# The first two mixers of a transformer stack: score and value products of two heads at once in halves of the matmul array

## The reference

```
p   = softmax(q k^T * scale, causal)              per head
o_a = g0 * p_cmp v_cmp + g1 * p_slc v_slc + g2 * p_win v_win
y_a = heads of o_a side by side;  y_b = heads of p_moba v_moba
merged = gate_a * (y_a @ w_up_nsa) + gate_b * (y_b @ w_up_moba)
x = x + g_m * (merged @ w_out)
```

## Time and profile before

| | |
|---|---|
| median of 3 runs | 2048.45 us (2046.79 to 2048.81) |
| profiled execution, its own time | 2048.88 us |
| its span in the profile | 2047.0 us |
| granted clock of TensorE, mean | 0.998 |
| loop of the first mixer, first score to the last transposes of y | 88.38 to 234.01 us |
| loop of the second mixer | from 531.41 us |

### The profile page before, as it was taken

How to read it: one execution, slowest core, us unless ns; L and a number is a source line. 1 busy time by engine, 2 the same in 40 slices (tenths; PEclk the granted TensorE clock), 3 DMA queues, 4 the chain that set the end, 5 groups by cost and what they waited for, 6 DMA issues and landing times. The chain is left out here.

```text
span 2047.0 us, 32169 instructions
## 1 busy us (share of the span) xinstructions
PE 1998.6 (98%) x12934; PEld 1775.0 (87%) x12934; DVE 1465.8 (72%) x2326; ACT 1093.2 (53%) x1732; POOL 23.6 (1%) x46
## 2 busy tenths in 40 slices
PE   7999999999999999999999999999999999999999
PEld 4889898898788988898888779888898899899888
DVE  7887778867786686567766676677667757767774
ACT  3555545535656455545545656655455536855552
POOL 1001000000010000000000000000000000000000
PEclk9999999999999999999999999999999999999999
DMA  9455458856455466555556324355555554235554
GB/s 353 157 205 196 167 181 275 273 207 187 145 201 211 147 224 206 185 186 185 186 190 201 125 102 144 130 187 187 186 177 187 186 181 137 93 124 163 187 175 134
DMA packets 266212, 372.23 MB, mean 182 GB/s; under 512 B 8400, under 2 KB 160336, under 8 KB 266064
## 3 DMA queue, kind: packets, MB, share of 16 engines
q1 hardware_dynamic: 264736, 368.91, 54.2%
q10 hardware_dynamic: 1328, 1.26, 0.2%
HBM read 369.09 MB, written 1.05 MB: 181 GB/s over the span
## 5 line engine op out<-in xcount | busy, mean ns | idle before, releaser
L2302 DVE TENSOR_TENSOR parts<-ring,parts 128x2048 fp32r<-128x2048 f32 (+2 forms) x304 | 675.8, 2223 | 396.1 <-ACT parts L721 395.4
L721 ACT ACTIVATE parts<-ring 128x2048 fp32r<-128x2048 f32 (+2 forms) x304 | 565.5, 1860 | 560.9 <-PE psum L1513 317.0
L1513 PE MATMUL psum<-h,parts 128*128 128x512 f32 x1920 | 675.9, 397 | 0.0
L1511 PE MATMUL psum<-h,parts 128*128 128x256 f32 x1920 | 539.0, 281 | 0.7 <-DVE parts L2302 0.5
L1513 PEld LDWEIGHTS psum<-h,parts 128*128 128x128 f32 x1920 | 360.6, 188 | 87.0
L1511 PEld LDWEIGHTS psum<-h,parts 128*128 128x128 f32 x1920 | 362.3, 189 | 2.5 <-DVE parts L2302 2.3
L1505 PE MATMUL psum<-h,parts 128*128 128x256 f32 (+1 forms) x2088 | 265.0, 285 | 4.5 <-DVE h L2311 2.0
L1505 PEld LDWEIGHTS psum<-h,parts 128*128 128x128 f32 (+1 forms) x2088 | 253.9, 190 | 7.3 <-issue 5.0
L1505 PE MATMUL psum<-parts,h 128*128 128x512 f32 (+1 forms) x864 | 204.9, 388 | 5.2 <-DVE h L2311 2.9
L1505 PE MATMUL psum<-hid_hl,parts 128*128 128x256 f32 x1584 | 189.4, 281 | 0.8 <-DVE parts L2302 0.6
L1505 PEld LDWEIGHTS psum<-hid_hl,parts 128*128 128x128 f32 x1584 | 188.0, 188 | 2.4 <-DVE parts L2302 2.4
(11 more groups left out here) (265 smaller groups left out, 2116.7 us busy)
## 6 DMA issues: line engine op xcount, KB each, us to landing
ring<-in_w_ffn_in SPq DMA_DIRECT2D x88, 512.0 KB, 4.8
ring<-in_ffn_w_gate SPq DMA_DIRECT2D x88, 512.0 KB, 3.7
ring<-in_ffn_w_up SPq DMA_DIRECT2D x88, 512.0 KB, 4.7
ring<-in_w_ada SPq DMA_DIRECT2D x43, 1024.0 KB, 5.4
ring<-in_w_in SPq DMA_DIRECT2D x36, 1024.0 KB, 5.0
ring<-in_ffn_w_down SPq DMA_DIRECT2D x32, 1024.0 KB, 4.9
ring<-in_w_ffn_out SPq DMA_DIRECT2D x16, 1024.0 KB, 5.1
ring<-in_ffn_w_down SPq DMA_DIRECT2D x16, 768.0 KB, 4.5
```

Of the source, the lines that this page charges most:

```text
L721: act.activation(out, in_, func, **kw).then_inc(*sig(name, *keys))
L1511: pe.matmul(bank[:, 0:S], wt_hl[1], act[:, 0, :], start=start, stop=False, skip_group_check=True)
L1513: return pe.matmul(bank.rearrange("p (a s) -> p a s", a=2), wt_hl[0], act, start=False, stop=stop, skip_group_check=True)
L2302: dve.tensor_tensor(out, a, b, op).then_inc(*sig(name, *keys))
```

## The change

- **Scores.** `scores_pair` takes two heads in every even round, one with its rows in the upper 64 partitions, one in the lower, each in its own bank, and alternates them piece by piece. Scores, turned probabilities and the small transposes now share four banks (0, 1, 6, 7).
- **Values.** `weighted_pair` makes the values stationary (128*64) and moves the turned probabilities: 256 columns for the first 128 keys, 128 for the last. Two heads write to the two halves of the output partitions. Up to head 15 four heads are done in one go every fourth round; after that two in every second.
- **Normalisation.** DVE makes a factor for each head (reciprocal of the row sums, times the gate) and ACT multiplies the probabilities by it (`scaled`) before the transposes. All three branches of y_a then gather in one accumulator (banks 4 and 5), y_b in banks 6 and 7, already in the layout of the next projection: `branch`, `moba_out`, the copy of the compressed branch and all transposes of y go.
- **Order.** Transposes come three rounds after the scores instead of two; the loop has 28 rounds. Score and probability buffers rotate by four. The compressed output moves from round 6 to round 11. In round 23 ACT first copies the last two gate banks and then runs both sigmoids over 2048 columns.

```diff
-HEADS, LAG, UNITS = 24, 2, 2
+HEADS, LAG, LATER, UNITS = 24, 2, 3, 2
...
-        scores_area = sb("scores_area", [P, 5, 512])
-        shifted = scores_area[:, 0:3, :]
-        prob_t = scores_area[:, 3:5, :]
+        scores_area = sb("scores_area", [P, 8 * 384])
...
+        in_mixer = scores_area[:, :].rearrange(
+            "p (a n) -> p a n", n=384)
...
+        def shifted_of(st, n):
+            return in_mixer[:, n % 4, :] if tiled(st) else shifted[:, n % 3, :]
+
+        def prob_of(st, n):
+            return in_mixer[:, 4 + n % 4, :] if tiled(st) else prob_t[:, n % 2, :]
...
-            for j in range(4):
-                for g in range(2):
-                    n = 4 * g + j
...
+            for n in (0, 4, 1, 5, 2, 6, 3, 7):
+                g, j = divmod(n, 4)
...
+        def turned_place(bank, n):
+
+            half, c = HD * (n % 2), S * (n // 2 % 2)
+            return psum[half:half + HD, bank + n // 4, c:c + S]
...
+            def scaled(head, n):
+
+                st, i = head["st"], head["i"]
+                buf = shifted_of(st, n)
+                act.wait_ge(*at(("factor", st, i)))
+                for t, (a, b) in enumerate(spans(head["mask"])):
+                    run(buf[:, a:b], buf[:, a:b], ACT.Copy, "act_scaled", ("scaled", st, i, t),
+                        scale=factor[:, n % 4, t:t + 1])
...
-                                act.wait_ge(*at(("copied", ("gbr", l, 5))))
-                                run(br_gates[:, 1, 0:4], br_gates[:, 1, 0:4], ACT.Sigmoid,
-                                    "act_step")
                                 for q in (6, 7):
...
+                                    copies(("gbr", l, q), br_e[:, 2 * q:2 * q + 2, :])
+                                act.wait_ge(*at(("copied", ("gbr", l, 7))))
+                                for a in range(2):
+                                    run(br_gates[:, a], br_gates[:, a], ACT.Sigmoid, "act_gates",
+                                        ("gates", l, a))
                                 act.preload_act_table_set(EXP_LN)
...
+                    if LATER <= i < HEADS + LATER:
+                        m = i - LATER
+                        turned_copy(heads[m], base + m)
+                    if i < HEADS:
+                        exps(heads[i], base + i,
+                             heads[i]["n"] + (8 if heads[i]["st"][0] == "win" else 0))
+                    if 1 <= i <= HEADS:
+                        scaled(heads[i - 1], base + i - 1)
...
-                    if i == 22:
+                    if i == 20:
                         for j in range(2):
                             y_copies(("tr y", l, 0, j), 2 * j, y_mix)
-                    if i == 25:
+                    if i == 24:
                         y_copies(("tr y", l, 1, 0), 4, y_mix)
...
+                def scores_pair(i, pool):
...
+                    for t, (a, c) in enumerate(spans(pair[0]["mask"])):
+                        for head, job, b in zip(pair, jobs, banks):
+                            mm = pe.matmul(b[:, a:c], head["q"][:, P * t:P * t + P],
+                                           head["k"][:, 0:c - a], start=True, stop=True)
+                            if t:
+                                mm.then_inc(*sig("pe_scores", ("full", job)))
...
+                def weighted_pair(which, first, done):
+
+                    pair = [heads[i] for i in which]
+                    pe.wait_ge(*at(("copied", ("turn", pair[1]["st"], pair[1]["i"]))))
+                    probs = [prob_of(head["st"], base + i) for i, head in zip(which, pair)]
+                    for t, (a, c, q0) in enumerate(((0, S, 0), (S, S + P, P))):
+                        for n, head in enumerate(pair):
...
+                            mm = pe.matmul(head["o"][:, q0:S], head["v"][t], moving,
+                                           start=first and t == 0, stop=t == 1,
+                                           skip_group_check=True)
...
-            def moba_turn(l, j):
-                transposes(("tr y", l, 1, j), [y[:, 1, t, P * (2 * j + a):P * (2 * j + a) + P]
...
+                def weighted_of(i):
+
+                    if i >= 16:
+                        if i % 2:
+                            weighted_two((i - 1, i), i % 8 // 2)
+                    elif i % 4 == 3:
+                        for g in range(2):
+                            weighted_two((i - 3 + g, i - 1 + g), 2 * g + i % 8 // 4)
...
+                def compressed_out():
...
+                    for c in range(4):
+                        pe.matmul(psum[:, 4 + c // 2, S * (c % 2):S * (c % 2) + S],
+                                  v_diag[:, P * c:P * c + P],
+                                  cmp_pt.rearrange("p t q -> p (t q)"), start=False, stop=True,
+                                  skip_group_check=True)
...
-                for i in range(HEADS + LAG + 1):
-                    if i < HEADS:
-                        scores(i)
-                    if LAG <= i < HEADS + LAG:
-                        turn(i - LAG)
+                for i in range(HEADS + LATER + 1):
+                    if i < HEADS and i % 2 == 0:
+                        scores(i, ATT + (SIDE if i < 22 else (4, 5)))
+                    if LATER <= i < HEADS + LATER:
+                        turn(i - LATER, ATT + (SIDE if i < 21 else ()))
...
-                    if i > LAG:
-                        weighted(i - LAG - 1)
+                    if i > LATER:
+                        weighted_of(i - LATER - 1)
...
-                    if i == 6:
-                        pe.wait_ge(*at(("copied", ("cmp turn", l))))
-                        pe.wait_ge(*at(("v diag", l)))
-                        for t in range(TT):
-                            b = open_bank(("cmp out", l, t), SIDE)
-                            pe.matmul(b, cmp_pt[:, t, :], v_diag, start=True, stop=True).then_inc(
-                                *sig("pe_out", ("full", ("cmp out", l, t))))
+                    if i == 11:
+                        compressed_out()
...
-                    if i == 21:
-                        for j in range(2):
-                            transposes(("tr y", l, 0, j),
...
                     if i in ADA_AT and pending:
-                        ada_cols(*pending.pop(0), SIDE if i < 10 else (4, 5))
+                        ada_cols(*pending.pop(0), ATT + SIDE if i < 20 else (4, 5))
...
-                def moba_out(p, pv):
...
-                def branch(b, kind):
...
+                def scaled(i):
...
+                    dve.wait_ge(*at(("probs", st_, head["i"], 1)))
+                    total, out = sums[:, column, :], factor[:, (base + i) % 4, :]
+                    done = ("factor", st_, head["i"])
+                    if st_[0] == "moba":
+                        dve.reciprocal(out, total).then_inc(*sig("dve_step", done))
+                    else:
+                        dve.reciprocal(out, total).then_inc(*sig("dve_step"))
                         settle()
+                        tt(out, out, gate[:, :, head["n"], 1 if st_[0] == "slc" else 2],
+                           ALU.mult, "dve_step", done)
...
                     if i < HEADS:
                         masked(heads[i]["st"], heads[i]["i"], con("causal"), HD ** -0.5)
+                    if 1 <= i <= HEADS:
+                        scaled(i - 1)
...
-                    if i == 7:
-                        for t in range(TT):
-                            job = ("cmp out", l, t)
-                            dve.wait_ge(*at(("full", job)))
-                            dve.tensor_copy(y[:, 0, t, :], psum[:, tally.bank(job), :]).then_inc(
-                                *sig("dve_freed", ("free", job)))
-                    if i == 11:
-                        branch(1, "slc")
-                    if i == 19:
-                        branch(2, "win")
```

More of the change, by code:

```diff
@@ L1704, in scores, with turn @@
                     mm.then_inc(*sig("pe_scores", ("full", job)))
-                def turn(i):
+                def scores_pair(i, pool):
+                    for key in (scores_need or {}).get(i, ()):
+                        pe.wait_ge(*at(key))
+                    pair = heads[i:i + 2]
+                    jobs = [("scores", head["st"], head["i"]) for head in pair]
+                    banks = [open_bank(job, pool) for job in jobs]
+                    for t, (a, c) in enumerate(spans(pair[0]["mask"])):
[4 more added lines that the diff above has]
+                                mm.then_inc(*sig("pe_scores", ("full", job)))
+                def turn(i, pool=ATT):
                     head = heads[i]
                     job = ("turn", head["st"], head["i"])
-                    b = open_bank(job, ATT)
-                    buf = shifted[:, (base + i) % 3, :]
+                    b = open_bank(job, pool)
+                    buf = shifted_of(head["st"], base + i)
+                    kind = "scaled" if tiled(head["st"]) else "probs"
```

(18 more changed lines are left out.)

149 lines of the change are left out of this document (55 added, 94 removed).

## The result

The change makes the kernel slower: 2081.71 us (median of 5 runs, 2079.33 to 2090.87) against 2047.73 for the kernel before on the same chip (5 runs), a ratio of 1.0175 [1.0150, 1.0199]. The forecast was 2032 us. The profiled execution has a span of 2089.0 us; it is the slowest of the five (2090.87 us, 9 above the median), so rows from it show somewhat more loss than a typical execution has.

What follows compares the result with a forecast made beforehand. PE was taken as the bound (98% busy), DVE next in rounds 0 to 13. Terms 8.0+0.7+1.8+0.9-2.5-0.7 give 8.2 us a layer, 16.4 for two, hence 2032 us; range 2019 to 2046.

Steps and rivals of the forecast that it cites:

- the prediction's own signs: Marks in PE's timeline: scores group outside 1.0 to 1.5 us refutes the forecast; waits over 5 us a layer mean DVE's term was too small.
- Scores, 8.0 us: Scores of two heads in row halves: 0.67 us saved a pair, 12 pairs, 8.0 us a layer (ends 11.8 and 4.1).
- if starts stay in order: Scores of a pair: only one head's last instruction lies beside the other's first, so the stream is taken as 0.95 us.
- The upper end of 11.8: Scores term if the two heads' halves run wholly side by side: 11.8 us saved a layer.
- Values, 0.7: Values of two heads in column halves: 14.2 us becomes 13.5, 0.7 saved a layer (ends +4.4 and -3.3).
- The prediction's visit of 0.26: Values: each of eight visits to the column halves costs about 0.26 us (0.10 in, 0.05 load, 0.10 out).
- Transposes of y, 1.8: PE's 16 transposes of y a layer, 0.11 us each, go: 1.8 us saved.
- the compressed wait, 0.9: PE's wait for the copy of the compressed probabilities goes, as the compressed output moves five rounds later: 0.9 us saved a layer.
- The new link, -2.5: Rounds 0 to 13: DVE's 64 us of work nearly fills PE's shortened span; loss between 0 and 7.8, taken as 2.5 a layer.
- four banks help little: Rounds 0 to 13: pairs, small transposes and w_ada columns all draw on the banks, so they barely relieve a late DVE.
- The tail, -0.7: End of the mixer: gate-bank wait halves to about 1 us, a 2.3 us wait behind the sigmoids comes; 0.7 lost a layer.
- the slower rival: `scaled` makes DVE wait for ACT's exponentials, 1.5 us a round: 6.2 us lost a layer, 2061 us; chance 0.14 with anything else slower.

Runs made afterwards that it cites:

- e11_pair_less: Number 5 with two of four multiply-adds of each w_ada panel left out on DVE in the two mixers; 2012.73 us, ratio 0.9823.
- number 12: The changed kernel with each pair's scores written head by head instead of alternating piece by piece; 2082.38 us, ratio 1.0163.
- number 1: The changed kernel with separate banks for scores, for transposed probabilities and small transposes, and for the compressed branch; 2052.03 us, ratio 1.0012.
- numbers 8 to 10: 8: number 5 with one head's scores every round, 2041.29 us; 9: number 5 with half the w_ada multiply-adds, 2012.73; 10: 8 with that same cut, 2029.35.
- Number 6: The changed kernel with idle bf16 products put into two of PE's waits in each mixer; 2075.81 us, ratio 1.0136.
- number 4: The changed kernel with DVE's low part of the second w_up_nsa panel made before the first unit of mix_a again; 2074.15 us, ratio 1.0123.
- number 5: The changed kernel with pools apart, sigmoids later, compressed keys copied a round earlier and DVE's dropped split restored; 2034.86 us, ratio 0.9929.

## Why the prediction was wrong

The products gained more than forecast; what was missed is what the code around them does to PE. Two of the prediction's own signs show it: the scores group takes 0.85 us, below its 1.0, and PE's new waits are far over 5 us a layer. An account for one mixer of the profiled execution, from the stretches: PE's work falls by about 18.9 us (152.1 before; afterwards 133.2, which is the 134.5 of e11_pair_less less 38% of the 3.4 us that it still ran at half clock); the half clock adds 15.3 (148.5 against 133.2); idle time grows by 23.1 (28.0 against 4.9). The sum is the measured +19.5, as it must be by the way the terms are formed. A typical execution (number 12, first mixer) has 12.7 for the clock (145.9 against 133.2) and 23.0 of idle time, +16.8 in all.

- **Scores, 8.0 us: too small.** 12 x (1.96 - 0.85) = 13.3. The failing step is "if starts stay in order": number 12 shows that one head's instructions don't hold up the other's, whichever are written first. The upper end of 11.8 was too low as well: it kept 0.34 for changes of shape on top of 0.64, where a pair makes do with 0.85 in all.
- **Values, 0.7: too small** by the same step, as far as the starts tell; no run puts the old values back. Four visits with four heads at 1.45 and four with two at 0.80 are 9.0 us, so 14.2 - 9.0 = 5.2. (The prediction's visit of 0.26 is 0.25 by its own items, which changes nothing.) The rule of the Trainium skill (TensorE: Matmul & The Clock Gate, Part 3: Packing small matmuls) that was weighed there, under which loads of column halves come into the open and the term is -1.7, is contradicted by the 1.45 us. Its other rule, of starts some 4 ns apart, holds in kind: here one half of a pair begins 6 to 7 ns behind the other.
- **Transposes of y, 1.8, and the compressed wait, 0.9**: nothing speaks against them; there are no transposes from y in the mixer and no wait in front of the moved output.
- **The new link, -2.5: the step that turned the sign.** The prediction saw that pairs, small transposes and w_ada columns share the four banks, and wrote "four banks help little". It took the worst case to be the loss of the gain in these rounds, 7.8, because it bounded the loss by DVE's total work. But DVE was idle in pieces: its 60.5 us fit well into 81.5. The rotation makes PE wait for a certain job of DVE while others come ahead of it, so idle time of both adds up. Pools apart were worth 30 us (number 1). Rounds 0 to 13 then take 69.8 us, near the 68.8 that the prediction had, and numbers 8 to 10 show that DVE does limit them.
- **The clock: not in the sum at all.** Every wait was priced at its own length. What PE then ran slower was another 15.3 us a mixer in the profiled execution and 12.7 in a typical one. Number 6 shows it as a cost of its own.
- **The tail, -0.7: too small.** The wait of 2.3 behind the sigmoids came (2.6). PE's 2.0 for the gate bank, which was to halve, is still 1.96: ACT starts the copies that free the last gate banks only at 224.31, behind the exponentials of the last head, before which it waited 1.5 us for nmax. The hunk on DVE's split was not costed: 5.96 us and its half clock, 8 to 11 us in all (number 4). In number 5 the tail is 33.6 against 31.1.
- **DVE waits for ACT's exponentials**, the slower rival: not what happened. DVE waited for them once in the first mixer, 1.0 us. Its price was wrong for the same reason as the forecast: one mechanism on DVE, no thought of PE's banks.

With the split restored, the pools apart and ACT's two jobs moved the idea gives 6.8 us a mixer, where the sum had 8.2, and 2034.86 us, where it had 2032. This agreement is partly by chance: the products saved 8 us a mixer more than forecast (18.9 against 8.0 + 0.7 + 1.8), and waits and clock took that.

What is open: which part of the remaining loss in rounds 0 to 13 is ACT's (the 2.7 us on the squares of round 4) was not tried by itself, nor were the values put back to the old order.

## What to carry to other kernels

Before a pool of buffers is shared among users, write out who draws in which order in the busiest round, and for each draw, who must have let go of the bank and what stands ahead of that on its engine. If that release is one round late, the reader's whole round becomes the writer's wait, whatever the shares of busy time say. Then price a new wait of TensorE with the half clock that may follow it, and read each hunk of a diff that moves a due time, even when it looks like bookkeeping.

## What was not expected of the hardware

- Float32 products in two row halves or in two column halves overlap all but 6 to 7 ns, and their weight loads do too; for row halves the written order of the two heads doesn't matter (number 12). Starts of one pair as the trace has them (us; engine; shape; both heads):

```
137.841  PE    64x256   137.844  PEld  64x128
137.848  PE    64x256   137.850  PEld  64x128
138.060  PE    64x256
138.066  PE    64x256
133.605  PE   128x128   133.606  PEld  128x64
133.611  PE   128x128   133.613  PEld  128x64
```

- A wait of 2.0 us was followed by 10.2 us at the lower clock, in which a pair of units took 4.83 us in place of 3.01. The same wait at the same place in number 12 was followed by 3.4 us of it, and the wait of 2.0 us in the tail of the kernel before by none.
